# Sliding attention filled with projection units of the other token half, in an eight-head hybrid block on one core

## The reference

```python
h = rmsnorm(x, norm_pre)
pool_u, pool_gate, q, k, v, attn_gate = split(h @ w_in)      # widths 512 512 512 128 128 512
pool_out = pool_mixer(pool_u, pool_w, pool_scale) * silu(pool_gate)
attn_out = swa_sink_attention(q, k, v, sinks) * silu(attn_gate)
y = concat([pool_out, attn_out]) @ w_out
x = x + rmsnorm(y, norm_post)
```

## Time and profile before

| | |
|---|---|
| median of three runs | 1938.94 us (1932.54 to 1939.75) |
| the profiled execution | 1934.91 us, its span 1933.1 us |
| mean granted TensorE clock | 0.967 of 2.4 GHz |
| PE busy | 1803.2 us (93%), 9240 matmuls |
| weight loads on PE | 1539.8 us (80%) |
| DVE busy | 868.6 us (45%) |
| ACT busy | 575.9 us (30%) |
| POOL busy | 487.1 us (25%) |
| DMA | 144.54 MB, mean 75 GB/s |

### The profile page before, as it was taken

One profiled execution on the slowest core, in us unless ns is written; L12 is line 12 of the kernel. 1 busy time (PEld: TensorE's weight loads), 2 busy tenths in 40 slices (PEclk: granted clock), 3 DMA queues, 4 the chain that ended last, 5 costly groups with the idle time before them and its releaser, 6 DMA issues. The chain is left out here.

```text
span 1933.1 us, 23184 instructions
## 1 busy us (share of the span) xinstructions
PE 1803.2 (93%) x9240; PEld 1539.8 (80%) x9240; DVE 868.6 (45%) x1389; ACT 575.9 (30%) x1316; POOL 487.1 (25%) x330
## 2 busy tenths in 40 slices
PE   4999899897999999999899999989998899999998
PEld 3777798676877777889888998967777688888776
DVE  4140477326601214532255313432325699994733
ACT  4101244124310114420144102421113576661111
POOL 6232300314322220112202022022312233434330
PEclk8999899798999999999999999999999799999999
DMA  6012200325132110011101011054334112106432
GB/s 198 19 65 69 73 1 1 116 83 153 48 133 82 44 37 19 22 57 44 44 18 54 20 44 49 24 163 135 116 136 163 40 36 69 37 20 212 142 120 87
DMA packets 86923, 144.54 MB, mean 75 GB/s; under 512 B 26656, under 2 KB 36512, under 8 KB 86688
## 3 DMA queue, kind: packets, MB, share of 16 engines
q10 hardware_dynamic: 56752, 86.55, 13.1%
q1 hardware_dynamic: 30064, 56.50, 9.9%
HBM read 104.30 MB, written 38.73 MB: 74 GB/s over the span
## 5 line engine op out<-in xcount | busy, mean ns | idle before, releaser
L515 POOL TENSOR_SCALAR w_hi<-w_stage 128x1024 fp32r<-128x1024 f32 (+4 forms) x123 | 129.4, 1056 | 1155.1 <-PEq L787 525.2
L519 POOL TENSOR_TENSOR w_lo<-w_stage,w_hi 128x1024 fp32r<-128x1024 f32 (+4 forms) x123 | 271.7, 2213 | 9.3
L782 PE MATMUL ps<-w_hi,h2T_hi 128*128 128x512 f32 x584 | 251.7, 431 | 2.2 <-issue 1.6
L782 PE MATMUL ps<-w_lo,h2T_hi 128*128 128x512 f32 x584 | 238.3, 408 | 0.0
L782 PE MATMUL ps<-w_hi,h2T_lo 128*128 128x512 f32 x584 | 238.1, 408 | 0.0
L1776 DVE TENSOR_TENSOR rope_cos_part<-ps,cos_dil 128x512 f32<-128x512 f32 x48 | 33.2, 692 | 374.4 <-PE ps L782 297.0
L782 PEld LDWEIGHTS ps<-w_hi,h2T_hi 128*128 128x128 f32 x584 | 161.7, 277 | 15.7 <-issue 5.1
L782 PEld LDWEIGHTS ps<-w_hi,h2T_lo 128*128 128x128 f32 x584 | 161.9, 277 | 10.6
L782 PEld LDWEIGHTS ps<-w_lo,h2T_hi 128*128 128x128 f32 x584 | 162.9, 279 | 9.3
L540 PE MATMUL ps<-h2T_hi,w_hi 128*128 128x512 f32 x384 | 153.8, 400 | 4.8 <-ACT gate_tiles L1245 2.4
L540 PE MATMUL ps<-h2T_hi,w_lo 128*128 128x512 f32 x384 | 152.4, 397 | 0.0
(11 more groups left out here) (265 smaller groups left out, 3595.6 us busy)
## 6 DMA issues: line engine op xcount, KB each, us to landing
w_stage<-in_w_in SPq DMA_DIRECT2D x76, 512.0 KB, 3.7
w_stage<-in_w_out SPq DMA_DIRECT2D x16, 512.0 KB, 3.7
gate_scr<-gate_tiles ACTq DMA_DIRECT2D x16, 512.0 KB, 2.9
gates<-gate_scr ACTq DMA_DIRECT2D x32, 256.0 KB, 4.0
dil_scr<-dil_out ACTq DMA_DIRECT2D x24, 264.0 KB, 2.1
dil_nums<-dil_scr ACTq DMA_DIRECT2D x24, 256.0 KB, 3.6
x_tiles<-in_x ACTq DMA_DIRECT2D x8, 512.0 KB, 8.6
x_back<-in_x ACTq DMA_DIRECT2D x8, 512.0 KB, 3.6
```

The costliest lines, as they stand in the source:

```text
L515: last = nc.gpsimd.tensor_scalar(hi_, raw_, 1.0, 0.0, ALU.mult, ALU.add)
L519: last = nc.gpsimd.tensor_tensor(lo_, raw_, hi_.bitcast(F32), ALU.subtract)
L782: m = pe.matmul(ps[:, u % 2, :], toks(a, k), b[:, s, k, :], start=(k == 0 and b is wh and a is h2h), stop=(k == KT - 1 and a is h2l))
```

## The change

- Panels: kv stands before q. The vectors are loaded by SP behind its fourth chunk, the pool's constants by SP behind its tenth chunk once x is transposed.
- x and u: the second token half's transposes are done in pairs of units between the u units of the first half; ACT and DVE follow in that order.
- Memory: the pool's result is written over `uT`; q, h1 and the mixer's high and low rows have places that let them live together; the mixer's rows are no longer behind a barrier.
- Order before the loop: kv (4 units), q for the first token half (4 units) with the v transposes between, attention gate for the first token half (4 units, `FILL`).
- The loop: the scores' heads are reordered so that neighbours alternate between the two key heads (`swa_head`), and PSUM is shared out anew: values have one bank, back transposes one, fill units two. Steps 0 to 7 carry half a unit of q for the second token half, 8 to 11 a unit of the gate for the second half, 12 to 18 parts of the output projection of tiles 0 to 2. ACT applies Silu to the gate. The mixer's rows are split tile by tile (attention) or slice by slice (pool, back by DMA one step ahead) in the loop.
- Output projection: one tile and half at a time in banks `Y_BANKS`; the first half's x1 transposes stand between its units, three c units in front of the second half's.
- Positions: three DMAs and one of frequencies.
- The barriers around the output projection are gone.

```diff
+def swa_head(slot):
+    hh, j = divmod(slot, G)
+    return G * (j // 2) + 2 * hh + j % 2
...
     add("pgate", panel(w1, 512))
+    add("kv", panel(w1, 1536, 256))
     add("q", panel(w1, 1024))
-    add("kv", panel(w1, 1536, 256))
...
+    Y_BANKS = (6, 0, 2, 4)
+    POOL_AT = (2, 4, 6, 8, 12, 13, 14, 15)
+    FILL = (("agate", 0), ("q", 1), ("agate", 1))
...
 # SP, behind chunk n
+                if n == STAGE + 2:
+                        for dst, vec in consts:
+                            sp.dma_start(dst, vec).then_inc(sem("const"), 16)
+                if n == STAGE + 8:
+                    sp.wait_ge(*after("x_T", 16))
+                    sp.dma_start(pool_wt[:], pool_w[0].rearrange("g c d -> c g d")).then_inc(sem("pool_c"), 16)
+                    for g in range(4):
+                        sp.dma_start(edge[:, g, :], ...).then_inc(sem("pool_c"), 16)
...
 # PE
-        transposes_in(xt, "x", 4)
+        transposes_in(xt, "x", 0, range(KT), upper)
...
                 wide_unit("u", ps[:, b, :], hTh, hTl, n, plain_cols(g)).then_inc(sem("u_done"), 1)
+                if n == 0:
+                    transposes_in(xt, "x", 1, (2 * g, 2 * g + 1), upper)
...
+        for u in range(5):
+            qkv_unit(u)
         pe.wait_ge(*after("mix_evac", 8))
         for half in range(2):
+            pe.wait_ge(*after("qkv_evac", 3 + half))
...
+        for u in range(5, 8):
+            qkv_unit(u)
+        for f in range(4):
+            fill_unit(f, 0)
+            fill_unit(f, 1)
...
 # scores
-            for j in range(G):
-                h = G * hh + j
+            for j in (0, 2, 1, 3):
+                h = swa_head(G * hh + j)
...
 # values
-            if i >= 2:
-                pe.wait_ge(*after("swa_out", i - 1))
+            if i >= 1:
+                pe.wait_ge(*after("swa_out", i))
...
+        in_loop = {i: ((4 + i // 2, i % 2),) for i in range(8)}
+        in_loop.update({i: ((i, 0), (i, 1)) for i in range(8, 12)})
+        out_loop = {12: ((0, 0, 0),), 13: ((0, 0, 1),), 14: ((0, 1, 0),), 15: ((0, 1, 1),),
+                    16: ((1, 0, 0), (1, 0, 1)), 17: ((1, 1, 0), (1, 1, 1)), 18: ((2, 0, 0), (2, 0, 1))}
         for i in range(steps + 3):
             if i < steps:
                 swa_scores(i)
-            if 2 <= i < steps + 2:
+            if 2 <= i < steps + 2 and i != steps + 1:
                 swa_values(i - 2)
-            if i < steps:
-                attn_gate(i)
+            for unit in in_loop.get(i, ()):
+                fill_unit(*unit)
+            for unit in out_loop.get(i, ()):
+                out_part(*unit)
...
+        for t, half in ((2, 1), (3, 0), (3, 1), (4, 0), (5, 0), (6, 0)):
+            out_unit(t, half)
+        pe.wait_ge(*after("y_read", 4))
+        transposes_in(xt2, "x1", 0, range(4), odd)
+        out_unit(7, 0)
+        pe.drain().then_inc(sem("panel_used"), 1)
+        transposes_in(xt2, "x1", 0, range(4, KT), odd)
+        for t in range(4, TT):
+            out_unit(t, 1)
...
+        for t in range(3):
+            c_unit(t)
+        pe.wait_ge(*after("y_read", TT))
+        transposes_in(xt2, "x1", 1, range(KT), odd)
+        for t in range(3, TT):
+            c_unit(t)
...
 # ACT
+        def pool_in(u):
+            n, k = divmod(u, 4)
+            if u >= 2:
+                act.wait_ge(*after("pool_lo", u - 1))
+            act.dma_start(pmR[:, u % 2, :], pool_d[P * k:P * k + P, COLS * n:COLS * n + COLS]).then_inc(sem(f"pool_back{u % 2}"), 16)
...
-                act.wait_ge(*after("ag_done", i + 1))
-                act.activation(sgA[:, i % 2, :], ps[:, 7, 0:2 * P], ACT.Exp, scale=-1.0).then_inc(sem("ag_evac"), 1)
-            if i >= 1:
+            if 1 <= i <= steps:
                 swa_pT(i - 1)
-        phase_end(act, "act")
+            if i in POOL_AT:
+                pool_hi(POOL_AT.index(i))
+            if i + 1 in POOL_AT:
+                pool_in(POOL_AT.index(i + 1))
+            if i < 8 and i % 2:
+                fill_evac(4 + i // 2)
+            if 8 <= i < 12:
+                fill_evac(i)
+            if i >= 5 and i % 2:
+                attn_hi((i - 5) // 2)
...
 # DVE
             if 2 <= i < steps + 2:
                 normalise(i - 2)
+            if i - 1 in POOL_AT:
+                pool_lo(POOL_AT.index(i - 1))
+            if i >= 6 and i % 2 == 0:
+                attn_lo((i - 6) // 2)
             if i >= 4 and i % 2 == 0:
                 back((i - 4) // 2)
-            if i < steps:
-                gate_attn(i)
-        phase_end(dve, "dve")
```

More of the change, by code:

```diff
@@ L69, in constants @@
     swa = np.where(valid[:, None, :], -slopes[None, :, None] * dist[:, None, :], np.float32(NEG))
+    swa = swa[:, [swa_head(i) for i in range(H1)]]
     j = np.arange(MASK_W)[None, :]
@@ new lines, in out_part @@
+        def out_part(t, half, part):
+            name = ("o0", "o1")[half]
+            s = index[name] % 2
+            tk = slice(P * t, P * t + P)
+            if part == 0:
+                if t == 0:
+                    panel_ready(name)
+                if t in (0, 4) and half == 0:
+                    pe.wait_ge(*after("pool_lo", t + 4))
+                pe.wait_ge(*after("attn_lo", t + 1))
+                if t == 0:
+                    pe.wait_ge(*after("fill_evac", 11 + half))
+                elif t == 1:
+                    pe.wait_ge(*after("swa_masked", steps))
+                elif t == 2:
+                    pe.wait_ge(*after("swa_pT", steps))
+                elif t == 3:
+                    pe.wait_ge(*after("swa_out", steps))
+                    pe.wait_ge(*after("swa_aT", TT))
+                elif half == 0:
+                    pe.wait_ge(*after("y_read", t - 3))
+                else:
+                    pe.wait_ge(*after("x1_evac", t + 1))
+            for k in range(KT // 2 * part, KT // 2 * (part + 1)):
+                for j, (a, b) in enumerate(((mTh, wh), (mTh, wl), (mTl, wh))):
+                    m = pe.matmul(ps[:, Y_BANKS[t % 4] + half, :], a[:, k, tk], b[:, s, k, :],
+                                  start=(k == 0 and j == 0), stop=(k == KT - 1 and j == 2))
+            if half == 1 and part == 1:
+                m.then_inc(sem("y_done"), 1)
@@ L1081, in _ @@
                            ACT.Copy).then_inc(sem("u_evac"), 1)
+        for t in range(4):
+            x_root(t)
+        act.wait_ge(*after("gain_in", 16))
+        for k in range(KT):
+            x_hi(0, k)
+        for t in range(4, TT):
+            x_root(t)
+        for g in range(4):
+            u_evac(g)
+            x_hi(1, 2 * g)
+            x_hi(1, 2 * g + 1)
+        for u in range(4, 8):
+            u_evac(u)
         for u in range(8):
@@ L1167, in x1_root, with x1_hi @@
             act.activation(ssq2[:, t:t + 1], ssq2[:, t:t + 1], ACT.Sqrt, scale=1.0 / D, bias=EPS_C).then_inc(sem("x1_root"), 1)
+        def x1_hi(n):
+            for k in range(KT):
+                u = n * KT + k
+                act.wait_ge(*after("x1_T", u + 1))
+                act.activation(h2h[:, k, COLS * n:COLS * n + COLS], ps[:, Y_BANKS[u % 4] + 1, :], ACT.Copy,
+                               scale=gain_2[:, k:k + 1]).then_inc(sem("x1_hi"), 1)
         x_back(0)
@@ L1560, in _ @@
         nc.vector.memset(EPS_C, EPS).then_inc(sem("zeroed"), 1)
+        for g in range(4):
+            nc.vector.memset(uT[:, g, 0:PAD], 0.0)
         dve.wait_ge(*after("gain_in", 16))
```

357 lines of the change are left out of this document (172 added, 185 removed).

## The result

The changed kernel takes 1886.20 us (median of 4, 1881.52 to 1892.65) against 1937.81 us before (median of 4, 1932.54 to 1939.75): a ratio of 0.974, 95% interval 0.9719 to 0.9760. The forecast was 1881, range 1868 to 1900. Its profiled execution is the fastest of the four, 1881.52 us with a span of 1879.7 and a mean clock of 0.980; by that execution the sum, 1879.2, was off by 2.3 us. One execution of the kernel before, at 4379.80 us, and one of experiment 1, at 9761.20 us, belong to a slow state and are left out of every ratio.

What follows compares the result with a forecast made beforehand. PE was taken as the bound, 93% busy, with unfilled seams at a lower clock. 369.1 us became 319.2, 49.9 less; with the startup's 5.8, 55.7 off 1934.9 gave 1879.2, taken as 1881; range 1868 to 1900.

Steps and rivals of the forecast that it cites:

- Startup: Before the pool gate: u starts after the first token half's transposes; gain 5.8 us, bounds 0 and 14.
- Constants, q panel's split, v transposes: Before the loop: constants on SP's queue cost 0, POOL's q panel split cost 0, v transposes between q units 1.0 us.
- Loop: Attention steps and tail: 137.7 us of PE work plus 3 for POOL's contention, 140.7 in all.
- POOL's contention: Loop's late steps: POOL's o1 panel split slows DVE; 3 us added, bounds 0 and 12; 1 by the skill's rule.
- The scores' form: Attention loop: scores alternating between partition halves, a bank each, take 1.18 us in place of 1.92; gain 11 us.
- scores do not overlap: Rival 2, attention loop: the new scores' form brings nothing; +11 us, 1892; chance 0.08.
- The loop's ends and the seam: Gain 25 us at the loop's two ends with lower clock and barrier, 14 at the seam at 448.5 before c.
- Gates: Behind c: PE's 2.37 us wait for the gates' evacuations stays; cost 0, bounds -2 and +8.
- The positions' term: Before the gates: four small loads, about 6 us in place of 16, make DVE's angles and ACT's last c evacuation meet.
- Clock 1.00 from 100 to 440: Sign that the forecast holds: PE's clock at its full rate from 100 to 440 us.
- Rivals: Loop chain-bound, 1905 (0.13); scores not overlapping, 1892 (0.08); startup and gates give nothing, 1900 (0.09); slower, 1945 (0.03).
- the fourth: Rival 4, loop: pool tiles returning through ACT's queue delay the exps; 8 x 7 = 56 us, beyond it slower, 1945; chance 0.03.

Runs made afterwards that it cites:

- experiment 1: Changed kernel with the scores' old form (a step's four heads share one key row group): ratio to before 0.9815; runs 1895.80, 1896.33 and 1901.87 us.
- experiment 4: Changed kernel with all 16 groups of x transposes ahead of the first u unit again: median 1893.12 us, ratio to before 0.9788.
- experiment 2: Kernel before with only the scores' new head order and what belongs to it: 1937.33 us against 1934.96, ratio 1.0008 (0.9987 to 1.0029).
- experiment 8: Changed kernel profiled again, then with step 7's last q evacuation moved ahead of the transposed probabilities in ACT's queue: the latter 1884.60 us.

## Why the prediction was right, and where its steps were not

By stage the kernel took 0.6 us less than summed in the startup, 1.1 less from there to the loop, 2.1 more in the loop and 1.3 less from the output to c. The signs offset each other, so that the 55.7 summed and the 56.7 measured up to the gates differ by 1.0; that they lie so close is in part luck.

- **Startup**, predicted 5.8, measured 6.4 (87.58 against 93.97). The first u matmul came at 26.5, the wait for the last low parts was 1.83 where 1.9 stood. But 4.3 are the order's; the other 2.1 came from the x tiles, which were scaled earlier than the earlier trace rows has it, while POOL waited for a chunk that the constants' loads held back (experiment 4). The prediction gave that move no effect. For the wait on those tiles 0.84 was measured against 2.6.
- **Constants, q panel's split, v transposes**, predicted 0, 0 and 1.0 of PE's work: no wait for any of them in the trace; POOL split the q panel from 132.0 to 151.4, before kv ended.
- **Loop**, predicted 140.7, measured 142.8 (201.34 to 344.1). The steps came out within 0.1 us of the sum (6.84 and 7.28 where 6.75 and 7.2 stood; 9.65 to 10.1 in steps 9 to 11; the one wait of 1.1 behind them). These tenths, with two waits of 0.26 in front of the transposes, make 1.9 of the 2.1. Two terms were off besides, and they nearly cancel. The wait of 1.69 at step 8 was not foreseen: I asked whether ACT was free for pT, and not what stood behind pT in its queue. POOL's contention was put at 3 and cost 1.5:

```profile
293.29 1.22 DVE L1756 TENSOR_REDUCE attn_stats<-probs 128x4 f32<-128x1024 f32 x1
294.54 2.18 DVE L1757 TENSOR_TENSOR attn_stats<-attn_stats,small 128x4 f32<-128x4 f32 x1
...
301.82 0.16 DVE L1757 TENSOR_TENSOR attn_stats<-attn_stats,small 128x4 f32<-128x4 f32 x1
302.02 2.38 DVE L1758 TENSOR_TENSOR attn_stats<-attn_stats,small 128x4 f32<-128x4 f32 x1
```

  A sum of 128 x 4 values, 0.16 us alone, stood 2.2 us behind POOL's subtraction (294.31, 2.39 long), while the bias from PSUM kept its 1.22 and the maximum its 1.22. The rule of the Trainium skill that the prediction quotes (SBUF — State Buffer, Who interferes with whom) sorted these rightly, and the 1 us worked out by it was nearer than my 3.
- **The scores' form**, "11 us" and "scores do not overlap" as a rival. The size is near (9.7 in experiment 1), the reason was incomplete: of the prediction's steps this one did not hold by itself. I took a PE without waits as proof that PE set the pitch of 7.65 and 8.09. It did, by 0.05 us; the ring over DVE and ACT was as long. I read the mask sum at 283.30 as "right behind the scores"; those were done at 282.29, and what it stood behind was DVE's product for the gate, at 282.96. The ring's length was not asked for, and the pairing alone changes the time by -2.5 to +5.6 us (the interval of experiment 2). The loop's gain belongs to the pairing and to the gate's move off DVE together, and the prediction gave the second no share. Had the change kept the gate's work on DVE, the sum would by this reading have been wrong by about as much.
- **The loop's ends and the seam**, 25 and 14. The output units in the loop are worth 18.6 and the three c units 9.6 when each is taken back alone, clock included. The rest of the two terms is the barrier and the mixer's split, which no experiment took back.
- **Output to c**, predicted to end near 453, measured 451.6.
- **Gates**, cost 0: the wait is 2.38 as before, and 56.7 us were gained up to it against 55.7 summed. The positions' term was right only as to the gates. Their place in front of c's copies, which I put at 1 us, would have cost 11.7 with the old loads: the three DMAs are what makes the seam's gain possible, and I had looked at them for the angles alone.
- **Clock 1.00 from 100 to 440** holds in the profile that was read, and not in most executions: the 4.7 us by which the median lies above that profile are what one fall at step 8 can cost. That the two are the same is not shown, and experiment 8 speaks against it in part: without that fall the median is only 1.7 lower.
- **Rivals.** None came. For the fourth, the pool tiles: PE never waited for them.

## What to carry to other kernels

A PE that never waits does not say how near the next limit is. Before pricing an edit that shortens PE's step, add up the ring through the other engines in the order of their queues; where both come within a few per cent, the edit pays only together with one that shortens the ring. When work is moved to a place where PE now follows closely, read again what stands in the other engines' queues there: small DMAs that a barrier had hidden, and copies behind copies, become waits. And a wait of 1 to 2 us inside a busy stretch can cost three times its length up to the end of its stage, because the clock can fall behind it; in the whole time of this kernel that much did not show.

## What the runs showed of the hardware

- The granted clock fell from 1.00 to 0.50, from 2.4 to 1.2 GHz, behind a single idle time of 1.69 us in a stretch in which PE was 92% busy before it (7.37 of 8.00 us) and 100% behind it, in six of seven profiles. It stayed there for 7 to 10 us and cost 3.1 to 4.7.
- Scores of 64 x 256 whose neighbours use different halves of the partitions and different banks start their followers after 1.18 us a group of four; all in one half, 1.92. Halves and banks were changed together, so which of them does it is open.
- A VectorE sum of 128 x 4 values can take 2.2 us instead of 0.16 when GpSimd subtracts two SBUF tiles at that moment.
- Each small DMA costs ScalarE's queue 0.48 us here (24 in 11.44), 0.54 before (24 in 12.97).
